# Two mixing layers: latent blocks kept on chip and normed inside the projection, gates made inside the stage of the input rows, decays turned 512 columns at a time

## What is computed

```python
h = rmsnorm(x, mix_norm[l])
proj = h @ w_in[l]          # c_q 384, c_kv 256, k_pe 64, hq 512, hf 512, hi 512, hg 512
c_q, c_kv, k_pe, hq, hf, hi, hg = split(proj)
# latent attention: both latents are normed before they are projected up
q  = rmsnorm(c_q, q_a_norm[l]) @ w_q_b[l]
kv = rmsnorm(c_kv, kv_a_norm[l]) @ w_kv_b[l]
# gated recurrence: a gate and a log decay out of hf, the values are hi
q_g   = silu(hq)
f     = lb + (1 - lb) * sigmoid(hf)
log_f = log(maximum(f, 1e-30))
k_g   = (1 - lb) * sigmoid(-hf)
x = x + concat([attention(q, kv, k_pe), recurrence(q_g, k_g, hi, log_f) * silu(hg)]) @ w_out[l]
```

## Time and profile before

| | us |
|---|---|
| median of 3 runs | 6429.93 (6414.22 to 6430.46) |
| profiled execution, its own time | 6421.55 |
| span of its trace | 6419.3 |
| PE busy / PEld busy | 5425.8 (85%) / 4614.3 (72%) |
| DVE busy / ACT busy | 2788.1 (43%) / 2176.7 (34%) |
| granted clock of TensorE, mean | 0.908 |
| `gates` to `decay_rows` of layer 0 (1691.0 to 1726.2) | 35.1 |
| `load_down` and `mla_norms` of layer 0 (1898.5 to 1938.6) | 40.1 |

### The profile page before, as it was taken

How to read it: one execution, slowest core, us unless ns; L and a number is a source line. 1 busy time by engine, 2 the same in 40 slices (tenths; PEclk the granted TensorE clock), 3 DMA queues, 4 the chain that set the end, 5 groups by cost and what they waited for, 6 DMA issues and landing times. The chain is left out here.

```text
span 6419.3 us, 98155 instructions
## 1 busy us (share of the span) xinstructions
PE 5425.8 (85%) x38340; PEld 4614.3 (72%) x38341; DVE 2788.1 (43%) x4337; ACT 2176.7 (34%) x3244; POOL 363.4 (6%) x574
## 2 busy tenths in 40 slices
PE   6964776859688969999796789499999999999994
PEld 5653764648564559999675546398989899998994
DVE  2695333441352345555315323244444455554444
ACT  2212113532332334444323233133333444444432
POOL 0111000000140000000003100100000000000001
PEclk8986997979888979999898789599999999999997
DMA  2110001022000155555210001644444455554544
GB/s 76 40 46 2 2 15 58 21 106 67 14 20 17 44 220 205 187 207 206 105 48 5 30 7 61 221 169 159 157 160 153 170 186 192 192 186 183 190 153 170
DMA packets 112169, 713.81 MB, mean 111 GB/s; under 512 B 12960, under 2 KB 16816, under 8 KB 70320
## 3 DMA queue, kind: packets, MB, share of 16 engines
q1 hardware_dynamic: 96208, 657.53, 28.2%
q0 software_dynamic: 9184, 28.49, 1.3%
q10 hardware_dynamic: 6528, 24.12, 0.9%
HBM read 639.42 MB, written 70.67 MB: 111 GB/s over the span
## 5 line engine op out<-in xcount | busy, mean ns | idle before, releaser
L2843 DVE TENSOR_TENSOR experts_low<-experts_raw,experts_high 128x1024 fp32r<-128x1024 f32 x678 | 810.6, 1223 | 1007.7 <-ACT experts_high L2772 1007.7
L2707 PE MATMUL ps<-experts_xs_high,experts_high 128*128 128x256 f32 (+1 forms) x3584 | 1038.5, 290 | 40.0 <-issue 38.9
L2707 PE MATMUL ps<-experts_xs_high,experts_low 128*128 128x256 f32 (+1 forms) x3584 | 1041.0, 290 | 0.0
L2707 PE MATMUL ps<-experts_xs_low,experts_high 128*128 128x256 f32 (+1 forms) x3584 | 1037.4, 289 | 0.0
L2707 PEld LDWEIGHTS ps<-experts_xs_high,experts_high 128*128 128x128 f32 x3584 | 680.1, 190 | 52.6 <-issue 43.3
L2772 ACT ACTIVATE experts_high<-experts_raw 128x1024 fp32r<-128x1024 f32 x678 | 687.8, 1049 | 63.5 <-DMA experts_raw<-experts 63.5
L2707 PEld LDWEIGHTS ps<-experts_xs_low,experts_high 128*128 128x128 f32 x3584 | 681.4, 190 | 8.8
L2707 PEld LDWEIGHTS ps<-experts_xs_high,experts_low 128*128 128x128 f32 x3584 | 681.2, 190 | 0.0
L2391 PE MATMUL ps<-dense_xs_parts,dense_high 128*128 128x256 f32 x2816 | 498.9, 280 | 4.1 <-DVE dense_xs_parts L2494 2.7
L2391 PEld LDWEIGHTS ps<-dense_xs_parts,dense_high 128*128 128x128 f32 x2816 | 436.5, 189 | 12.5 <-issue 4.9
L2699 PE MATMUL ps<-experts_high,experts_hid_high 128*128 128x512 f32 x1120 | 444.8, 397 | 0.0
(11 more groups left out here) (514 smaller groups left out, 9259.1 us busy)
## 6 DMA issues: line engine op xcount, KB each, us to landing
experts_raw<-experts SPq DMA_DIRECT2D x226, 1536.0 KB, 6.5
dense_raw<-dense SPq DMA_DIRECT2D x90, 1536.0 KB, 6.4
proj_raw<-w_in SPq DMA_DIRECT2D x41, 512.0 KB, 3.6
y_slot<-route_blank SPq DMA_DIRECT2D x15, 1152.0 KB, 20.3
out_proj_raw<-w_out SPq DMA_DIRECT2D x48, 256.0 KB, 2.8
proj_keys_raw<-w_in SPq DMA_DIRECT2D x20, 512.0 KB, 3.6
x_mixed<-x_out SPq DMA_DIRECT2D x16, 512.0 KB, 4.8
y_slot<-experts_y ACTq DMA_DIRECT2D x8, 1024.0 KB, 8.7
```

The costliest lines, as they stand in the source:

```text
L2707: last = nc.tensor.matmul(ps[:, m, 0:width], w[:, u, m, c], x[:, k, 0:width], start=(k == 0 and i == 0), stop=(k == KD - 1 and i == 2))
L2843: nc.vector.tensor_tensor(low[:, v, t, :], raw[:, v % NR, t, :], high[:, v, t, :].bitcast(F32), ALU.subtract).then_inc(split, 1)
```

## The change

Three edits, in both mixing layers.

The six latent blocks are evicted to a tensor `down` that stays on chip; the spill, `load_down` and `mla_norms` are gone. `projections_and_norms` does the norms between its blocks of weights: ACT's squares behind the sixth block (`behind(0)`), DVE's pooling of the squares into one block per group, PE's sums behind the tenth block, ACT's roots and spreading behind the fourteenth, PE's transposes behind the sixteenth, and DVE's scaling after its last split. The room for the raw weights, the squares and the spread values is the first half of `mixT`, and `z` before it is written.

`inputs_and_gates` merges the stages `inputs` and `gates`: the gate work stands between the steps of rounding and subtracting in the lists of ACT and DVE, and DVE's copies of the banks come after the sum of the logarithms.

`decay_rows` turns four blocks into one bank of 512 columns, and ACT and DVE evict a bank each in turn.

```diff
-def norm_transpose(core, name, x, xT, gain, source, out=None):
+def norm_transpose(core, name, x, xT, gain, source, out=None, room=None):
...
-    junk = st.sb("junk", [P, 2, D])
     row = st.sb("gain", [P, D])
-    R = 3 if out is None else 4
-    xs = st.sb("scaled", [P, R, D])
...
     st.end()
-def gates_of_layer(core, name, l, qk, z):
...
-    small = st.sb("small", [P, 4, T])
...
+    widths = (384, 256)
+    squares = [room[:, 2, :], room[:, 3, :], z[:, 0, :], z[:, 1, :], z[:, 2, :]]
+    spread = [room[:, 2 + i, :].rearrange("p (b n) -> p b n", b=NT) for i in range(2)]
...
+            def behind(s):
+                if s == 1:
+                    for i, g in enumerate(groups):
+                        pe.wait_ge(pooled, (2, 3)[i])
+                        for b in range(NT):
+                            last = nc.tensor.matmul(core.ps[:, 4 + i, b:b + 1], squares[g[0]][:, b * P:(b + 1) * P],
+                                                    core.c("ones")[:, 0:1], start=True, stop=True)
+                        last.then_inc(sums, 1)
+                if s == 3:
+                    for i in range(2):
+                        pe.wait_ge(spreaded, i + 1)
+                        for b in range(NT):
+                            last = nc.tensor.transpose(two(4 + 2 * i)[:, b * P:(b + 1) * P], spread[i][:, b, :], core.c("eye"))
+                        last.then_inc(turned, 1)
+            blocks(pe, one, behind)
...
+            def one(n, u, seg, m, i):
+                if not isinstance(n, int) or n + 1 < total:
+                    if not isinstance(n, int) or n >= 1:
+                        act.wait_ge(product, n)
+                    round_block((n + 1 - (1 - u)) * 8 + 16, 1 - u)
+                act.wait_ge(product, n + 1)
+                nc.scalar.activation(seg[2](m), core.ps[:, 2 * u:2 * u + 2, :].rearrange("p a n -> p (a n)"),
+                                     seg[1]).then_inc(psum_free, 1)
+            def behind(s):
+                if s == 0:
+                    act.wait_ge(psum_free, 2 + segments[0][0])
+                    for b in range(5):
+                        nc.scalar.activation(squares[b], down[:, b, :], ACT.Square).then_inc(squared, 1)
+                if s == 1:
+                    act.wait_ge(sums, 2)
+                if s == 2:
+                    for i in range(2):
+                        act.wait_ge(meansq, i + 1)
+                        nc.scalar.activation(stat[:, 1, i, :], stat[:, 0, i, :], ACT.Sqrt).then_inc(rooted, 1)
+                    for i in range(2):
+                        act.wait_ge(inverse, i + 1)
+                        nc.scalar.activation(spread[i], stat[:, 2, i, :].unsqueeze(2).to_broadcast([P, NT, P]), ACT.Copy)\
+                            .then_inc(spreaded, 1)
+            blocks(act, one, behind)
...
+            first = segments[0][0] + 2
+            summed = segments[0][0] + segments[1][0] + 2
+            pairs(dve, first, lambda n, u, i: split_block(n, u))
+            for n, (a, b) in enumerate(((0, 1), (0, 2), (3, 4))):
+                dve.wait_ge(squared, b + 1)
+                if n == 1:
+                    dve.wait_ge(pooled, 1)
+                nc.vector.tensor_tensor(squares[a], squares[a], squares[b], ALU.add).then_inc(pooled, 1)
+            pairs(dve, summed, lambda n, u, i: split_block(n, u), first=first)
+            for i in range(2):
+                dve.wait_ge(sums, i + 1)
+                nc.vector.tensor_scalar(stat[:, 0, i, :], core.ps[:, 4 + i, 0:NT], 1.0 / widths[i], 1e-6,
+                                        ALU.mult, ALU.add).then_inc(meansq, 1)
+            for n in range(summed, summed + 3):
+                split_block(n, n % 2)
+            for i in range(2):
+                dve.wait_ge(rooted, i + 1)
+                nc.vector.reciprocal(stat[:, 2, i, :], stat[:, 1, i, :]).then_inc(inverse, 1)
+            for n in range(summed + 3, total):
+                split_block(n, n % 2)
+            for i, g in enumerate(groups):
+                dve.wait_ge(turned, i + 1)
+                for m, b in enumerate(g):
+                    nc.vector.scalar_tensor_tensor(down[:, b, :], down[:, b, :], core.v(gains[i], m), two(4 + 2 * i),
+                                                   ALU.mult, ALU.mult)
+    st.end()
+def inputs_and_gates(core, name, l, xT, weights, inputs, qk, z, small):
...
         @block.scalar
         def _(act):
+            def round_step(k):
+                act.wait_ge(loaded[k % 2], 16 * (k // 2 + 1))
+                if k >= 2:
+                    act.wait_ge(used, k - 1)
+                nc.scalar.activation(high[:, k % 2, :], raw[:, k % 2, :], ACT.Copy).then_inc(rounded, 1)
+            round_step(0)
+            round_step(1)
             act.wait_ge(shifted, 2)
             nc.scalar.activation(low[:, 2:4, :], low[:, 0:2, :], ACT.Exp).then_inc(exps, 1)
             nc.scalar.activation(wide(qk[:, 1]), wide(z), ACT.Sigmoid, scale=-1.0).then_inc(sig, 1)
+            round_step(2)
             act.wait_ge(sig, 1)
             nc.scalar.activation(wide(z), wide(z), ACT.Sigmoid).then_inc(sig, 1)
+            for k in range(3, 6):
+                round_step(k)
+            act.wait_ge(ready, 1)
+            nc.scalar.activation(wide(small), wide(small), ACT.Ln).then_inc(logs, 1)
+            round_step(6)
             act.wait_ge(ready, 2)
             nc.scalar.activation(wide(z), wide(z), ACT.Ln).then_inc(logs, 1)
-            nc.scalar.activation(wide(small[:, :, :]), wide(small[:, :, :]), ACT.Ln).then_inc(logs, 1)
+            round_step(7)
...
+            split_step(0)
+            split_step(1)
...
+            split_step(2)
+            split_step(3)
             dve.wait_ge(sig, 2)
             for j in range(4):
                 ts(qk[:, 1, j, :], qk[:, 1, j, :], low[:, 7, j:j + 1], None, ALU.mult)
                 last = ts(z[:, j, :], z[:, j, :], low[:, 7, j:j + 1], low[:, 6, j:j + 1], ALU.mult, ALU.add)
             link(last)
+            split_step(4)
             link(ts(wide(z), wide(z), 1e-30, None, ALU.max))
-            ts(wide(small[:, :, :]), wide(z), tiny, 1 / tiny, ALU.min, ALU.mult).then_inc(ready, 1)
+            split_step(5)
+            ts(wide(small), wide(z), tiny, 1 / tiny, ALU.min, ALU.mult).then_inc(ready, 1)
             dve.wait_ge(ready, 1)
             ts(wide(z), wide(z), tiny, None, ALU.max).then_inc(ready, 1)
+            split_step(6)
+            split_step(7)
             dve.wait_ge(logs, 2)
-            tt(wide(z), wide(z), wide(small[:, :, :]), ALU.add)
+            tt(wide(z), wide(z), wide(small), ALU.add).then_inc(decayed, 1)
+            dve.wait_ge(decayed, 1)
+            for b in range(NT):
+                dve.wait_ge(product, b + 1)
+                nc.vector.tensor_copy(inputs[:, b, :], core.ps[:, b, :])
+    st.end()
+def decay_rows(core, name, z, log_decays):
...
+        @block.tensor
+        def _(pe):
+            for b in range(NT):
+                for j in range(4):
+                    last = nc.tensor.transpose(core.ps[:, b, j * P:(j + 1) * P], z[:, j, b * P:(b + 1) * P], core.c("eye"))
+                last.then_inc(turned, 1)
+        @block.scalar
+        def _(act):
+            for b in range(0, NT, 2):
+                act.wait_ge(turned, b + 1)
+                nc.scalar.activation(log_decays[:, b, :], core.ps[:, b, :], ACT.Copy)
+        @block.vector
+        def _(dve):
+            for b in range(1, NT, 2):
+                dve.wait_ge(turned, b + 1)
+                nc.vector.tensor_copy(log_decays[:, b, :], core.ps[:, b, :])
     st.end()
+        down = sb("down", [P, 6, T])
...
-                norm_transpose(core, f"mix_norm{l}", as_rows(qk[:, :, :, :].rearrange("p a j n -> p (a j) n")), xT, f"mix_row{l}", source)
-                projections(core, f"proj{l}", d[f"w_in{l}"], xT,
-                            [(6, ACT.Copy, None, d["spill_down"]), (4, ACT.Silu, lambda n: at(qk[:, 0], n), None),
-                             (4, ACT.Copy, lambda n: at(z, n), None), (4, ACT.Silu, lambda n: at(mixT[:, 4:8], n), None)])
-                product_rows(core, f"inputs{l}", xT, KD, d[f"w_hi{l}"], 1, inputs)
-            gates_of_layer(core, f"gates{l}", l, qk, z)
+                norm_transpose(core, f"mix_norm{l}", as_rows(qk[:, :, :, :].rearrange("p a j n -> p (a j) n")), xT, f"mix_row{l}", source,
+                               room=mixT)
+                projections_and_norms(core, f"proj{l}", d[f"w_in{l}"], xT,
+                                      [(6, ACT.Copy, lambda n: at(down, n)), (4, ACT.Silu, lambda n: at(qk[:, 0], n)),
+                                       (4, ACT.Copy, lambda n: at(z, n)), (2, ACT.Silu, lambda n: at(mixT[:, 4:6], n)),
+                                       (2, ACT.Silu, lambda n: at(mixT[:, 6:8], n))],
+                                      down, mixT[:, 0:4, :], z, (f"qa{l}", f"kva{l}"))
```

(8 more changed lines are left out.)

102 lines of the change are left out of this document (100 added, 2 removed).

## The result

| | before | changed | ratio |
|---|---|---|---|
| median, 4 runs each, us | 6429.02 | 6316.00 (6303.05 to 6318.74) | 0.9825 [0.981, 0.9841] |
| profiled execution, its own time | 6421.55 | 6303.05 | |
| its span | 6419.3 | 6301.4 | |

The change is faster by 113 us, where 144 were forecast. The time lies outside the range, 11 us above its upper end. Two more series of the same kernel gave 6320.07 and 6311.34.

The account below looks back on a forecast made before the run. PE bounds `proj`; stages around it don't overlap, so each costs its whole length. Gains of 70.75 and 70.1 us, together 140.9 off 6421.55, give 6280.7, or 6289 from the median; forecast 6285, range 6266 to 6305.

Parts of the forecast that it names:

- The gates in the input rows: Part 1, merging `inputs` and `gates`: ACT and DVE do the gates while PE runs, giving back 34.7 us a layer.
- no PE wait in steps 4 to 7: Sign in the merged `inputs`: PE never waits for a late subtraction, with 2.3 us as the thinnest margin.
- the second Ln ahead of round 7: Sign in ACT's merged list of `inputs`: second Ln done at 40.0 us, round 7 at 40.7.
- The decays: Part 2, `decay_rows`: 32 transposes at the high clock take 4.4 us; 2.5 us a layer won, -0.3 if the clock falls.
- The stages removed: Part 3: `load_down` and `mla_norms` go, giving back 40.05 us in layer 0 and 39.45 in layer 1.
- What the projection takes on: Added PE work in `proj`, 16 one-column sums and 16 transposes: 6.5 us a layer, bounds 5.6 and 15.8.
- I take 6.5: The cost in us a layer taken for the sums and transposes added to `proj`, near the low bound.
- Each burst is short and follows matmuls at 0.99: Reason given for taking 6.5 us a layer in `proj`, near the low end of 5.6 to 15.8.
- The sum: Whole kernel: 70.75 us from layer 0 and 70.1 from layer 1, together 140.9 off 6421.55, gives 6280.7.
- if a stage outside the mixing layers changes its length: Sign, outside the mixing layers, that the prediction named as showing it wrong; no size given.
- Rival 1: Smaller gain: merged ACT and DVE lists stall PE in `inputs` and `proj`; 6295 to 6325 us, chance 0.14.
- Rival 3: Slower: sums in `proj` drop the clock through its last 8 blocks and `inputs`, 132 us a layer; 6550, chance 0.025.

Follow-up runs that it names:

- e3: The kernel before with only the latent blocks kept on chip and normed inside the projection, gates and decays as before: 6364.47 us, ratio 0.9888.
- e13: The changed kernel with an added stage of one semaphore increment on PE behind the first block, ahead of both mixing layers: 6298.67 us, ratio 0.9799.
- e9: The changed kernel with an added stage of one semaphore increment on PE directly ahead of the experts: 6291.82 us, ratio 0.9792.
- e8: The changed kernel with 4 matmuls of 512 columns against ones replacing 16 one-column sums and 16 transposes: 6281.87 us, ratio 0.9766.
- e1: The changed kernel run again unaltered, for the spread and a second profile: 6320.07 us, ratio 0.9822.
- e12: The changed kernel run again unaltered in a later series, as its control: 6311.34 us, ratio 0.9815.

## Why the prediction was wrong

**The gates in the input rows: right.** The lists ran as laid out, no PE wait in steps 4 to 7, and the second Ln ahead of round 7. The transposes start 51.0 us after SP's first load in both layers, 1.1 us a layer better than worked out.

**The decays: right in mechanism.** The clock was high and the transposes took 3.68 instead of the 4.4 of the sum. From PE's first transpose to ACT's first work in the next stage it is 5.09 and 5.36 us, where it was 8.94 and 8.50: 3.9 and 3.1 won, and 2.5 taken. That `inputs` to `up_q` as a whole came within 1.1 us of the forecast over both layers is in part luck: these two parts won 4.2 us more than forecast, and `gated` with `gated_norm` in layer 0, which the change doesn't touch, took 3.0 us more.

**The stages removed: right.** `inputs` to `up_q` fell by 40.2 and 41.5 in e3, against 40.05 and 39.45.

**What the projection takes on: the term "I take 6.5" was too small.** It measured 8.8 and 8.5 in the changed kernel, within its bounds of 5.6 and 15.8. The transposes at 1.8 and the first sums are near the low bound; the clock fell in the second half of the sums, which cost the rest. e13 shows this by itself, for in its layer 0 the clock didn't fall. Its windows there:

```profile
1552.00:1559.00 7.00, 7.00 (x49) 6.38 (x48) 0.00 (x0) 1.91 (x2) 0.00 (x0) 1.00 0.00 0
```

and its `proj` took 211.1, 5.4 more than before. So the work is 5.4 and the fall of the clock some 3.3. "Each burst is short and follows matmuls at 0.99" was no reason: short bursts did lower it. This is 4.3 us of the error.

**The sum: the step that failed.** "Together 140.9 off 6421.55" took the length of every stage that the change doesn't touch as fixed; the text named a change there only as what would make it wrong. The experts became 16.3 us longer, 12.3 of them in PE's waits for code at the heads of the passes; as far as the runs show, because the code ahead of them changed. The prediction's own list of signs had it: "if a stage outside the mixing layers changes its length". Nothing of this stands in the timeline of the mixing layers, but the warning was in the profile of before: pauses of 3.0, 3.0 and 8.2 us at the heads of equal passes, with nothing waited for, say that such a pause has several lengths and that the program doesn't choose. Where an added stage of one increment made two (e9) or one (e13) of the three long pauses short, the time was 6291.82 and 6298.67, both inside the range and 7 and 14 us above the forecast.

The mechanism behind the pause is only partly shown. PE waits for a transfer on the queue of instructions and goes on 1.9 to 2.2 us behind its end. The Trainium skill, page "Runtime: NRT & Kernel Launch", section "🔬 Instruction fetch mechanics", says that code comes in 16 KB blocks and that a taken branch outside what is held forces a fetch and a stall. By that rule the place of the loop's code within its blocks sets how many fetches a jump back waits for. The traces agree in the 16 KB of each transfer, in the stall at the jump back and in the pauses' going with the place; a long pause has one transfer more. Which place gives which pause, and why e9 and e13 differ, isn't shown by any run here.

**The attention: 8.1 us more, cause open.** The clock at two windows of the attention of layer 1, changed kernel:

```profile
3596.20:3783.50 187.30, 165.16 (x672) 95.61 (x672) 61.31 (x178) 65.95 (x140) 0.00 (x0) 0.82 0.01 3
```

and before:

```profile
3733.36:3915.39 182.03, 161.42 (x672) 93.42 (x672) 61.30 (x178) 66.04 (x140) 0.00 (x0) 0.84 0.01 3
```

The same 672 matmuls take 5.3 us longer at a mean clock of 0.82 than at 0.84. Over all profiles the length goes with the time at 0.50: 174.6 us with 37.5 of it, 182.0 with 58.0, 187.3 with 68.3. In layer 1 every kernel with the latents on chip had 187.2 to 187.4, but for e13 (184.5) and e8 (181.9), and those without had 182.0 or less. In layer 0 it differs between executions of one kernel: the three profiles of the changed kernel have 172.6, 178.2 (e1) and 181.5 (e12). What sets it wasn't tried.

Last, the forecast of 6285 stood 4.3 above the sum for a profiled execution, and the median measured stands 13.0 above its own: 8.7 more. The profiled execution was the fastest of the four. Those of e1 and e12 took 6310.92 and 6315.25, and of the 12.2 us between the first and the last, the attention of layer 0 has 8.9 and the experts 4.5, while other stages are a little shorter. So part of these 8.7 us, too, is likely in stages outside the change. With 23.0 from the stages (4.3 + 16.3 + 8.1 - 4.6 - 1.1), less 0.6 for what lies around the span, the 8.7 make the 31 us between forecast and result.

**The rivals.** Rival 1 forecast 6295 to 6319, and the time fell in it, but not by its mechanism: the merged lists stalled nothing. Rival 3's price was wrong, as the clock came back in seven microseconds.
